# Four gathered dots a head beside the ranking of an expert layer, and GpSimd's gathers between its low parts

## The reference, cut to what matters

```
q = (xf @ wq).reshape(n, PEER_HEADS, 2, PEER_HALF)            # 8 heads, 2 halves of 128
s = jnp.einsum('nhpd,hpkd->nhpk', q, subkeys)                  # 128 scores a half
s_top, i_top = lax.top_k(s, PEER_TOPK)                         # best 16 of each half
cand = s_top[:, :, 0, :, None] + s_top[:, :, 1, None, :]
best_s, best_j = lax.top_k(cand.reshape(n, PEER_HEADS, -1), PEER_TOPK)
expert = ...                                                   # 16 experts a head and frame
gate = jax.nn.softmax(best_s, axis=-1)
h = jnp.einsum('nd,nhkd->nhk', xb, u[eb])                      # dot with each picked row of u
coef = gb * jax.nn.gelu(h, approximate=False)
out = jnp.einsum('nhk,nhkd->nd', coef, v[eb])                  # weighted sum of picked rows of v
```

## Time and profile before

| | us |
|---|---|
| median of 3 runs | 2052.51 (2049.53 to 2053.21) |
| profiled execution, its own time | 2070.54 |
| its span, first to last instruction | 2068.8 |
| TensorE busy | 1919.1 (93%) |
| VectorE busy | 1532.9 (74%) |
| ScalarE busy | 764.1 (37%) |
| GpSimd busy | 609.5 (29%) |
| DMA, mean over the span | 201 GB/s |

### The profile page before, as it was taken

One profiled execution on the slowest core, in us unless ns is written; L12 is line 12 of the kernel. 1 busy time (PEld: TensorE's weight loads), 2 busy tenths in 40 slices (PEclk: granted clock), 3 DMA queues, 4 the chain that ended last, 5 costly groups with the idle time before them and its releaser, 6 DMA issues.

```text
span 2068.8 us, 34098 instructions
## 1 busy us (share of the span) xinstructions
PE 1919.1 (93%) x13250; PEld 1627.3 (79%) x13250; DVE 1532.9 (74%) x2826; ACT 764.1 (37%) x1113; POOL 609.5 (29%) x403
## 2 busy tenths in 40 slices
PE   5989998888999879999999999969999999999996
PEld 4978876348983349999999999957887877889995
DVE  6277994314446248999989999958787868879898
ACT  3222454442220033334346666533333333333332
POOL 2322343000000015555552222252222323235550
PEclk9988999787999989999999999989999999999998
DMA  3211232001005024434468988899999999999991
GB/s 125 72 62 41 92 112 72 0 1 43 3 4 203 0 85 152 137 131 140 147 240 295 319 313 322 306 380 356 345 369 354 348 319 351 356 317 339 377 356 68
DMA packets 173720, 416.53 MB, mean 201 GB/s; under 512 B 13953, under 2 KB 89217, under 8 KB 170385
## 3 DMA queue, kind: packets, MB, share of 16 engines
q1 hardware_dynamic: 119728, 256.16, 36.1%
q0 software_dynamic: 36864, 134.23, 17.2%
q10 hardware_dynamic: 16992, 24.26, 3.2%
HBM read 363.08 MB, written 51.51 MB: 200 GB/s over the span
## 4 chain that ended last, share of the span: by engine, by line
PE 40%; DVE 14%; DMA 6%; issue 1%; ACT 0%; SPq 0%; DVEq 0%; ACTq 0%
PE ps L2012 21%; PE ps L1927 11%; PE ps L1931 5%; DMA gates<-dense_gates 3%; PE ps L1985 3%; DVE is_place L2099 2%; DMA coef<-parked_gelu 2%; DVE is_place L2094 1%; DMA w_staged<-in_stream 1%; DVE picks L2102 1%; DVE top_at L2060 1%; DVE top_at L2069 1%; DVE s_head L2063 1%; DVE best_at L2060 1%; DVE best_at L2069 1%
## 5 line engine op out<-in xcount | busy, mean ns | idle before, releaser
L2012 PE MATMUL ps<-w_hl,coef_hl 128*128 128x512 f32 x2304 | 539.7, 395 | 23.5 <-DVE coef_hl L2186 23.5
L2012 PEld LDWEIGHTS ps<-w_hl,coef_hl 128*128 128x128 f32 x2304 | 436.8, 190 | 119.6 <-DVE coef_hl L2186 25.6
L1927 PE MATMUL ps<-h_hl,w_hl 128*128 128x384 f32 (+1 forms) x2304 | 447.8, 346 | 15.6 <-DVE h_hl L2032 8.7
L1927 PEld LDWEIGHTS ps<-h_hl,w_hl 128*128 128x128 f32 x2304 | 406.9, 190 | 30.2 <-issue 9.1
L1542 POOL DMA_INDIRECT gathered_rows<-in_u_rows,pick_index x128 | 161.6, 1262 | 379.1 <-DVE pick_hidden L1552 359.4
L1861 ACT ACTIVATE w_hl<-w_staged 128x1024 fp32r<-128x1024 f32 x143 | 152.2, 1064 | 246.7 <-PE ps L2012 153.5
L1542 POOL DMA_INDIRECT gathered_rows<-in_v,pick_index x128 | 168.5, 1316 | 239.9 <-DVE h_tok L1561 201.6
L1931 PE MATMUL ps<-h_hl,w_hl 128*128 128x384 f32 (+1 forms) x1152 | 230.0, 340 | 0.0
L1931 PEld LDWEIGHTS ps<-h_hl,w_hl 128*128 128x128 f32 x1152 | 203.3, 188 | 5.0
L1801 POOL TENSOR_TENSOR w_hl<-w_staged,w_hl 128x1024 fp32r<-128x1024 f32 x64 | 164.4, 2571 | 136.4 <-ACT w_hl L1826 111.9
L1561 DVE SCALAR_TENSOR_TENSOR h_tok<-gathered_rows,pick_hidden,h_tok 128x1024 f32<-128x1024 f32 x128 | 164.1, 1282 | 6.7 <-DVE h_tok L1561 0.5
(11 more groups left out here) (315 smaller groups left out, 2558.0 us busy)
## 6 DMA issues: line engine op xcount, KB each, us to landing
w_staged<-in_stream SPq DMA_DIRECT2D x132, 512.0 KB
h1T<-in_v SPq DMA_DIRECT2D x66, 512.0 KB
w_staged<-in_v SPq DMA_DIRECT2D x62, 512.0 KB
dense_gates<-lot SPq DMA_DIRECT2D x24, 1024.0 KB
gates<-dense_gates SPq DMA_DIRECT2D x16, 1536.0 KB
w_staged<-in_w_in_t SPq DMA_DIRECT2D x40, 512.0 KB
parked_gelu<-h1T ACTq DMA_DIRECT2D x102, 192.0 KB
coef<-parked_gelu SPq DMA_DIRECT2D x102, 192.0 KB
```

The source lines that it names most:

```text
L1927: nc.tensor.matmul(ps[:, bank, 0:width], w_hl[:, j % RING, 0, P * k:P * (k + 1)], h_hl[:, part, k, lo:SEQ], start=(k == 0 and part == 0), ...
L2012: last = nc.tensor.matmul(ps[:, 2 + 2 * t + half, :], coef_hl[:, k % HLS, c, P * t:P * (t + 1)], w_hl[:, s % RING, v, 512 * half:512 * (ha ...
```

## The change

The row numbers are made for each head at the end of its rank. GpSimd's 64 low parts are written out, and behind that of tile 6h + 11 stands a wait for head h's row numbers and its first four gathers. VectorE makes the four dots of head h - 1 behind the rank of head h (28 in all), and the last four ahead of the lots. The lots keep two dots each (numbered from 32 on now), the six tiles behind them have one each for three, and in the parked part 1.0 passes a step stand for 1.1. The loop over heads on VectorE is written out too.

```diff
-    DOTS_A_LOT, DOTS_BEHIND = 2, 3
-    used_behind = [DOTS_A_LOT * LOTS + DOTS_BEHIND * (n + 1) for n in range(BEHIND)]
+    DOTS_A_HEAD, DOTS_A_LOT, DOTS_BEHIND = 4, 2, 1
+    IN_LOTS = DOTS_A_HEAD * PEER_HEADS
+    used_behind = [IN_LOTS + DOTS_A_LOT * LOTS + DOTS_BEHIND * (n + 1) for n in range(BEHIND)]
     EARLY = used_behind[-1]
-    A_PARKED = 1.1
+    A_PARKED = 1.0
...
-            with pool.Fori(0, BY_POOL // 8) as i:
-                for j in range(8):
-                    low(i * 8 + j, j)
-            pool.wait_ge(gathering["picked"], 1)
-            for n in range(2 * PICKS):
+            for s in range(BY_POOL):
+                low(s, s)
+                h, m = divmod(s - PER_HEAD, PER_HEAD)
+                if 0 <= h < PEER_HEADS and m == PER_HEAD - 1:
+                    pool.wait_ge(gathering["picked"], h + 1)
+                    for n in range(DOTS_A_HEAD * h, DOTS_A_HEAD * (h + 1)):
+                        gather_rows(nc, pool, a, gathering, n)
+            for n in range(IN_LOTS, 2 * PICKS):
                 gather_rows(nc, pool, a, gathering, n)
...
-            with dve.Fori(0, PEER_HEADS // 2) as i:
-                rank(i, 0)
-                rank(i, 1)
+                v_.scalar_tensor_tensor(gathering["index"][:, K * h:K * (h + 1)], picks[:, 0, 0, K * h:K * (h + 1)],
+                                        float(EXPERT_KEYS), picks[:, 1, 0, K * h:K * (h + 1)], ALU.mult, ALU.add
+                                        ).then_inc(gathering["picked"], 1)
+
+                for n in range(DOTS_A_HEAD * (h - 1), DOTS_A_HEAD * h):
+                    if n >= 0:
+                        dot_rows(nc, dve, h_tok, gathering, n)
+
+            for h in range(PEER_HEADS):
+                rank(h)
...
-            v_.scalar_tensor_tensor(gathering["index"][:, :], picks[:, 0, 0, :], float(EXPERT_KEYS), picks[:, 1, 0, :],
-                                    ALU.mult, ALU.add).then_inc(gathering["picked"], 1)
...
+            for n in range(IN_LOTS - DOTS_A_HEAD, IN_LOTS):
+                dot_rows(nc, dve, h_tok, gathering, n)
+
...
-                for x in range(DOTS_A_LOT * n, DOTS_A_LOT * (n + 1)):
+                for x in range(IN_LOTS + DOTS_A_LOT * n, IN_LOTS + DOTS_A_LOT * (n + 1)):
                     dot_rows(nc, dve, h_tok, gathering, x)
```

More of the change, by code:

```diff
@@ L2041, in _, with rank @@
             dve.wait_ge(counted, 2)
-            def rank(i, r):
+            def rank(h):
+                r = h % 2
                 done = [0]
@@ L2071, in rank @@
                 dve.sem_clear(order_sem)
-                dve.wait_ge(s_copied, i * 4 + (2 * r + 2 + 4))
-                dve.sem_inc(order_sem, 1)
-                done[0] += 1
+                dve.wait_ge(s_copied, 2 * h + 2 + 4)
                 best_two_rounds(lambda x: s_head[:, r, x // NT, x % NT, :], lambda x: top[:, x // NT, x % NT, :],
@@ L2087, in rank @@
                 put(v_.tensor_scalar(split_at[:, 1], best_at[:, :], K - 1, None, ALU.bitwise_and))
-                put(v_.tensor_copy(picks[:, 2, :, bass.ds(i * (2 * K) + r * K, K)], best[:, :]))
+                put(v_.tensor_copy(picks[:, 2, :, K * h:K * (h + 1)], best[:, :]))
                 settle()
@@ L2101, in rank @@
                 settle()
-                put(v_.tensor_reduce(picks[:, 0:2, :, bass.ds(i * (2 * K) + r * K, K)], is_place[:, :], AX.X, ALU.add))
+                put(v_.tensor_reduce(picks[:, 0:2, :, K * h:K * (h + 1)], is_place[:, :], AX.X, ALU.add))
                 settle()
-            with dve.Fori(0, PEER_HEADS // 2) as i:
-                rank(i, 0)
-                rank(i, 1)
+                v_.scalar_tensor_tensor(gathering["index"][:, K * h:K * (h + 1)], picks[:, 0, 0, K * h:K * (h + 1)],
[6 more added lines that the diff above has]
+                rank(h)
             gate = picks[:, 2].rearrange("p t (h k) -> p (t h) k", h=PEER_HEADS)
-            v_.scalar_tensor_tensor(gathering["index"][:, :], picks[:, 0, 0, :], float(EXPERT_KEYS), picks[:, 1, 0, :],
-                                    ALU.mult, ALU.add).then_inc(gathering["picked"], 1)
             v_.tensor_copy(small[:, :], gate[:, :, 0]).then_inc(softmax_sem, 1)
```

## The result

| | before | after |
|---|---|---|
| median, us | 2052.86 (2049.53 to 2058.08) | 2087.1 (2081.63 to 2089.85) |
| ratio, 95% interval | | 1.0161 (1.0131 to 1.0191) |
| profiled execution | 2070.54 | 2081.63 |
| first rank begins | 796.2 | 785.3 |

The changed kernel is 34 us slower. The profiled executions differ by 11 only, and the last line says why they can't be subtracted: where the first rank begins, with nothing changed before it, they are already 11 us apart. So from here on times are counted from the start of each execution's first rank.

The account below looks back on a forecast made before the run. TensorE was taken to bound the kernel nearly everywhere, the DMA engines between lots and sums. 31 us lost less 13 and 4 returned makes 14 more: 2066.5 us, own range 2056 to 2077, wide range 2047 to 2090.

Parts of the forecast that it names:

- the DMA relief: Behind the lots and in the parked part: fewer gathers return 13 us before the first sum and 4 in the parked part.
- GpSimd's bursts behind four gathers: Ranking, sign of being right: lows of tiles 12, 18, ... 54 start behind four gathers; TensorE waits up to 5 us a head.
- the undisturbed products: VectorE's ranks, sign of being right: products near their least times, as GpSimd waits when the later products run.
- The last index: End of the ranking, sign of being right: index 7 at 1055 to 1065, forecast at 1059.9.
- the stand before the first sum: TensorE before the first sum, sign of being right: 3 to 6 us; above 10 us would mean no relief.
- The new wait on GpSimd: Ranking: lows queue behind GpSimd's wait for each index and its gathers, so TensorE is held up; 31 us lost, bounds 22 and 42.
- instead of 4.4 I take half a low, 1.2, for each: Seven later ranks: disturbance of VectorE by GpSimd's lows falls from 4.4 us a rank to 1.2, 8.4 in all.
- the clock behind the last stand: TensorE after its last stand in the ranking: slow work could cost 2.3 us; 1 taken.
- My upper bound of 53: Ranking: the hold-up of TensorE reaches 53 us if the disturbance stays as now, with index 7 at 1082.3.
- the lock stays: Rival, ranks: lows spread over the products, seven ranks keep 4.4 us each; loss 53, return 17, 2088.5 us; chance 0.16.
- GpSimd must have its six lows done: Argument against the lock rival: the lows, 14.4 us, end before GpSimd waits again; products come 21 us after a rank's start.
- My upper bound of 12: Parked part: at most 12 us return from ten fewer gathers; 4 taken, with 9.0 us of TensorE idle time read there.

Follow-up runs that it names:

- late rates kept: Changed kernel with three dots a tile behind the lots and 1.1 passes a step in the parked part, as before the change: 2097.4 us, ratio 1.0226.
- one tile rate alone: Kernel before with one number changed, one dot a tile behind the lots instead of three, no early dots: 2046.3 us, ratio 0.9971.
- second profile of before: The kernel before, run and profiled again with no edit: median 2049.8 us, ratio 0.9985; its profiled execution took 2052.3 us.
- wait alone: Changed kernel without the 32 early gathers and dots, GpSimd's eight waits kept with nothing behind them: 2037.1 us, ratio 0.9941 to the kernel before.
- the gathers between: Changed kernel with a head's four gathers one behind each of four low parts, not all ahead of them: 2096.7 us, ratio 1.0213 to the kernel before.

## Why the prediction was right or wrong

Right: the direction and its cause. GpSimd's wait binds, the transposes come late, and the DMA relief gives back less than that. The sum of what came back was good: before the first sum 13 forecast, 13.9 measured beside the early dots (against the late rates kept) and 12.7 without them (one tile rate alone); in the parked and fresh parts 4 forecast, 3.2 measured against the second profile of before (646.0 - 642.8 from first to last sum) and 2.1 against the late rates kept (644.9 - 642.8). The 2087.1 lies inside the wide range of 2047 to 2090, near its end, and outside the 2056 to 2077 that I gave the forecast itself.

Of the signs that I named, GpSimd's bursts behind four gathers, TensorE's waits for them (seven, 33.7 us in all) and the undisturbed products came. The last index (277.4 behind the first rank, where 1055 to 1065 meant 259 to 269), the transposes (310.4 for 294), the cast and the stand before the first sum (2.1 us for 3 to 6) did not come as named.

Wrong is a size: a slowdown of 14 was forecast and 34 measured. The term that failed is the one in "The new wait on GpSimd": "instead of 4.4 I take half a low, 1.2, for each". The place of the collision (the burst meets the cast and the candidate sums) was right, and the products were free as I said. But I priced a collision as one instruction's remainder, with 2.4 as its upper end. In a chain of lows with no gap it lasts to the end of the chain: 3.7 us in six ranks and 6.2 in one, 28.4 in all where I had 8.4. The Trainium skill ("SBUF — State Buffer", "Who interferes with whom") tells of a lock for the whole instruction, and the traces agree with that. It also has who issues first block the other, and this doesn't tell who gets the ports when both want them: the cast, due at 898.61, was passed by the fifth low of the burst, which began at 900.07, 1.5 us later. What the traces show is that GpSimd keeps the ports while its next instruction is ready, and that a low gets in between two of VectorE's dots. Small terms went the other way: index operations 0.18 and not 0.3, nearly no gaps, a first rank with 1.2 of disturbance and not 3.2. Together the last index operation ended 13.7 us later behind the first rank than forecast (277.4 against 263.7). Gathers beside dots (6.8 for 6.1) and the clock behind the last stand added 1.3, and the hold-up was 46 and not 31: 46.0 - 13.9 - 3.2 = 28.9, as the second profile of before and the one of after have it (2079.9 - 2050.6 = 29.3 in span). The medians differ by 34, with an interval of 27 to 39; where the other 5 arise is not shown, but both values lie in it.

My upper bound of 53 for the loss, with "the lock stays" as its rival, covered it; the rival's picture was not what happened, since its products were free. That its time, 2088.5, came within 2 us is in part luck: it put 4.4 us a rank on the products, and the cast took 4.1 a rank in their place. The argument against it ("GpSimd must have its six lows done") was right about the products and silent about the cast.

A second fault didn't hurt: I read the stands of the parked part (9.0 us, one of 4.65) from an execution that took 18 us more than the median. My upper bound of 12 for the return there rested on it; the 4 that I took did not need so much idle time.

What stays open: how much of the 43.7 us between the last reduce of "wait alone" (233.5) and of the changed kernel (277.2) each part has. 24 dots are 27.5 and the longer locks on the cast 23.0 (30.6 us for the eight casts against 7.6), together more than 43.7; where VectorE had waited for TensorE, a part is taken up, and no run took the dots away and left the gathers.

## What to carry to other kernels

Where VectorE and GpSimd share a lock, count what queues behind a wait: work that is held back comes out as a burst, and a burst of GpSimd without gaps shut VectorE out to its end. A wait that only regroups work can shorten the other engine's chain by itself (here by 29 us, which the total time didn't clearly show), if the regrouped work falls where the other engine doesn't need the lock; then fill the room that it makes and no more, which here held one dot a head and not two or four. And take a second profile of the kernel before, when its profiled execution lies outside the timed runs.

## What the runs showed of the hardware

- A chain of five GpSimd subtractions of 2.35 us, each ready when the last ended, kept VectorE's cast out for up to 6.2 us and a two-input operation for 3.7; with a gap or a gather behind it, one low was all that VectorE waited for (2.39 us in the earlier trace rows, a dot of 3.35 us with the gathers between).
- The lock works both ways, but not alike: a low of 2.4 us that met a row of dots took 3.25, because it waited for one dot only. The gathers' issues, 0.94 us with no dot beside them, took 1.70 and 1.97 beside dots, while the dots stayed at 1.22.
- Two profiles of one kernel agreed within 0.1 us from the first rank to the first sum (601.2 in both), and differed by 11 us before it and 7 behind it.
